# The first norm's weights as one row, spread over the partitions by TensorE

## The chip, the cores and the metric

The kernel runs on one core of one Trainium2 chip. The metric is the device time of one execution in microseconds (us), the median of several runs. The program is a whole two-layer encoder in float32; the change concerns its first 25 us.

## The reference

A trunk of two layers over 256 tokens of width 1,024. Ahead of the layers stands a layer norm with a weight and a bias per feature; each layer is a token mixer (one input projection, four groups of heads, one output projection) and a channel mixer (dense, then eight experts), each followed by a norm.

```python
def layer_norm(x, w, b):
    xf = x.astype(jnp.float32)
    mu = jnp.mean(xf, -1, keepdims=True)
    var = jnp.mean(jnp.square(xf - mu), -1, keepdims=True)
    y = (xf - mu) * lax.rsqrt(var + EPS) * w.astype(jnp.float32) + b.astype(jnp.float32)
    return y.astype(x.dtype)
...
    h = layer_norm(x, ln_in_w, ln_in_b)
    for l in range(DEPTH):
        mix = token_mixer(h, w_in[l], w_out[l], ...)
        h = layer_norm(DN_ALPHA * h + mix, ln1_w[l], ln1_b[l])
...
        h = layer_norm(DN_ALPHA * h + f, ln2_w[l], ln2_b[l])
    return h
```

## The kernel before

Each engine has its own program, written out by hand in one order; semaphores join them. `x` is two tiles of 128 tokens by 1,024 features, `h[:, t, :]`.

**The queue.** All loads of the start are issued by SP, one behind the other, with no wait between them: the two tiles of `x`, the first norm's weights (`load_ln(0)`: `lnb`, 128 partitions by 2,048 columns, 1,024 KB; the host has repeated the row of 1,024 weights and 1,024 biases for all 128 partitions), the identity (`cst[:, first]`, 64 KB), the first block of input weights (`load_win(0, 0)`, 2,048 KB), the parameters (`pr`), a part of the constants, the second block of input weights (`load_win(0, 1)`), the rest of the constants, and the third block.

**The first norm** (`layer_norm(0, ...)` on VectorE). Statistics of both tiles (`stats`, L1581 to L1584); GpSimd turns each variance into 1/deviation (L516). Then, for tile 0 and then tile 1: the centre, two instructions of 512 columns, h = (h - mean) * weight (L1595), and the scale, one of 1,024 columns, h = h * (1/deviation) + bias (L1599), which signals `h_ready`. Every later norm (n = 1 to 4) goes through the same code.

**TensorE** waits for the identity and then runs `keep_busy(10, 7)`, ten products of the identity with itself into a corner of bank 7, whose results nobody reads (the fillers, L527). Then `transposes_of_h(0)` (L551): for each tile, as soon as its `h_ready` is there, eight 128x128 transposes into two PSUM banks, `HT_BANK[0] + 2 * t` and the next; with `HT_BANK[0] = 0` these are banks 0 to 3. ScalarE copies each bank to `hT` (L1224, four copies). Then `mix_0()`: it waits for all four copies and runs `unit(0, 0)` (L619, 16 products of 256 columns with the first block of input weights, into bank 5), `unit(0, 8)` (L631 and L632: for each of eight slices a product with the 16 gate columns and one of 512 columns with the second block, into banks 4 and 6), and so on. A product in float32 has two records in the trace, one for each pass of its weights.

**ScalarE**, after its four copies, waits for the parameters and starts the chain of small instructions of the S5 group (L1230).

Of the kernel before, what the change touches and what calls it, by code (L numbers as in the profile page):

```python
# [15 lines left out]
ALU = mybir.AluOpType  # L16
# [4 lines left out]
D = 1024  # L21
# [35 lines left out]
WOUT_LOADS = ((1, 2), (2, 7))  # L57
OUT_ORDER = (3, 2, 0, 1)
TILES = ((0, 1), (1, 0), (0, 1), (1, 0), (0, 1))
HT_BANK = (0, 4, 0, 0)  # L60
LINE = 64
MAGIC = 12582912.0
TURN = 6.2831850
# [4 lines left out]
def columns(sizes):  # L68

    at, out = 0, {}  # L70
    for name, n in sizes:
        out[name] = (at, at + n)
        at += n
    return out, -(-at // LINE) * LINE


CONST, CONST_W = columns([
    ("decay", H * 3 * P), ("dft_c", 512), ("dft_s", 512), ("idft_c", 512), ("idft_s", 512),
    ("window", 512), ("rot_c", 128), ("rot_s", 128), ("mask_fw", P), ("mask_bw", P), ("before", P),
    ("iota", P), ("ident", P), ("ones", P), ("pos", 2 * L), ("pick", H * P),  # L80
    ("m0", 2), ("nm0", 2), ("halfpi", 1), ("lower", NE * NE)])
# [7 lines left out]
def trunk(nc, x, ln, const, par, w_in, w_out, ffn, moe, tab, out):  # L89
    ctx = ExitStack()  # L90
    with ctx:
        place_of = {}

        def sb(name, shape, dt=F32):
            tensor = ctx.enter_context(nc.sbuf_tensor(name, shape, dt))
            place_of[name] = nc.sbuf_base - 4 * math.prod(shape[1:])
            assert name in ("lead", "over") or place_of[name] % (4 * LINE) == 128
            return tensor

        def sem(name):  # L100
            return ctx.enter_context(nc.semaphore(name))
# [8 lines left out]
        h = sb("h", [P, TT, D])  # L110
        lnb = sb("lnb", [P, 2 * D])
# [43 lines left out]
        bank = [ctx.enter_context(nc.psum_tensor(f"bank{i}", [P, 512], F32)) for i in range(8)]  # L155

        def K(name, rows=P):
            a, b = CONST[name]
            return cst[0:rows, a:b]
# [5 lines left out]
        ident = K("ident")  # L165
# [63 lines left out]
        def sm(a, n):  # L229
            return small[:, a:a + n]  # L230

        mv = sm(0, 4).rearrange("p (t s) -> p t s", t=2)
        bst = sm(4, 24).rearrange("p (t c s) -> p t c s", t=2, c=2)
        var, rstd = sm(28, 2), sm(30, 2)
# [23 lines left out]
        s_id, s_cst, s_par, s_ln = sem("identity_in"), sem("const_in"), sem("params_in"), sem("ln_in")  # L258
# [7 lines left out]
        dch, ach, pch = sem("dve_chain"), sem("act_chain"), sem("pool_chain")  # L266
        ln_var, ln_rstd, h_ready, ht_ps, ht_ready = (
            sem("ln_var"), sem("ln_rstd"), sem("h_ready"), sem("ht_transposed"), sem("ht_ready"))
        mix_ready = sem("residual_psum")
        init = sem("init_done")  # L270

# [55 lines left out]
        def ln_home(n):  # L327

            return ret[:, :] if n == 2 else lnb[:, :]
# [34 lines left out]
        def _(sp):  # L364
# [26 lines left out]
            def load_ln(n):  # L391
                if n == 2:
                    sp.wait_ge(f_pm, 2)
                    sp.wait_ge(f_sq, 4)
                elif n == 4:
                    sp.wait_ge(e_uu, 2 * NC_E * 6)
                elif n:
                    sp.wait_ge(h_ready, 2 * n)
                sp.dma_start(ln_home(n), ln[n]).then_inc(s_ln, 16)

            for t in range(TT):
                sp.dma_start(h[:, t, :], x[t * P:(t + 1) * P, :]).then_inc(s_x[t], 16)
            load_ln(0)
            first = slice(*CONST["ident"])
            sp.dma_start(cst[:, first], const[:, first]).then_inc(s_id, 16)
            load_win(0, 0)
            sp.dma_start(pr[:, :], par[0]).then_inc(s_par, 16)
# [78 lines left out]
            for c in range(2):  # L486
                sp.wait_ge(o_ready, 2 + c)
                part = slice(c * 512, (c + 1) * 512)
# [32 lines left out]
        def _(pe):  # L521
            mm, tr = nc.tensor.matmul, nc.tensor.transpose

            def keep_busy(count, b):

                for _ in range(count):
                    mm(bank[b][:, 384:512], ident, ident, start=True, stop=True)  # L527
# [11 lines left out]
            def transposes_of_h(n):  # L539
                for i, t in enumerate(TILES[n]):  # L540
                    if n == 1 and i:
                        keep_busy(6, 4)
                    elif n == 3 and i:
                        keep_busy(5, 7)
                        logits(0)
                        keep_busy(7, 7)
                    pe.wait_ge(h_ready, 2 * n + i + 1)
                    for j in range(2):
                        for q in range(4):
                            k = 4 * j + q  # L550
                            ins = tr(bank[HT_BANK[n] + 2 * t + j][:, q * P:(q + 1) * P], h[:, t, k * P:(k + 1) * P],  # L551
                                     ident)
                        ins.then_inc(ht_ps, 1)
                    if n == 1:
                        pe.wait_ge(d_id, 1)
                        for hf in range(2):
                            mm(bank[2 * t + hf][:, :], alpha_id, h[:, t, hf * 512:(hf + 1) * 512],
                               start=True, stop=False)
# [487 lines left out]
                    pre(1, k)  # L1046

            pe.wait_ge(s_id, 16)
            keep_busy(10, 7)
            transposes_of_h(0)  # L1050
            mix_0()
            transposes_of_h(1)
# [154 lines left out]
        def _(ac):  # L1207
# [7 lines left out]
            def evacuate_h(n):  # L1215
                dst = ff_x[0] if n == 1 else hT
                for i, t in enumerate(TILES[n]):
# [4 lines left out]
                    for j in range(2):  # L1222
                        ac.wait_ge(ht_ps, 4 * n + 2 * i + j + 1)
                        act(dst[:, 4 * j:4 * j + 4, t * P:(t + 1) * P],  # L1224
                            bank[HT_BANK[n] + 2 * t + j][:, :].rearrange("p (q n) -> p q n", q=4), ACT.Copy
                            ).then_inc(ht_ready, 1)
# [339 lines left out]
        def _(ve):  # L1566
            tt, ts, stt = nc.vector.tensor_tensor, nc.vector.tensor_scalar, nc.vector.scalar_tensor_tensor
            count = [0]

            def link(ins):  # L1570

                count[0] += 1
                ins.then_inc(dch, 1)
                ve.wait_ge(dch, count[0])

            def layer_norm(n, src, ready):

                def stats(i, t):
                    for c in (OUT_ORDER[2 * i] % 2, OUT_ORDER[2 * i + 1] % 2) if n % 2 else range(2):
                        ready(i, t, c)  # L1580
                        ins = nc.vector.bn_stats(bst[:, t, c, :], src(t, c))  # L1581
                    link(ins)
                    link(nc.vector.bn_aggr(mv[:, t, :], bst[:, t].rearrange("p c s -> p (c s)")))
                    ts(var[:, t:t + 1], mv[:, t, 1:2], EPS, None, ALU.add).then_inc(ln_var, 1)  # L1584

                for i, t in enumerate(TILES[n]):
                    if n or i == 0:
                        stats(i, t)
                    if n == 0 and i == 0:
                        stats(1, TILES[0][1])  # L1590
                    if i == 0:
                        ve.wait_ge(s_ln, 16 * (n + 1))
                    for c in range(2):
                        part = slice(c * 512, (c + 1) * 512)
                        ins = stt(out=h[:, t, part], in0=src(t, c), scalar=mv[:, t, 0:1], in1=ln_home(n)[:, part],  # L1595
                                  op0=ALU.subtract, op1=ALU.mult)
                    link(ins)
                    ve.wait_ge(ln_rstd, 2 * n + i + 1)
                    stt(out=h[:, t, :], in0=h[:, t, :], scalar=rstd[:, t:t + 1], in1=ln_home(n)[:, D:2 * D],  # L1599
                        op0=ALU.mult, op1=ALU.add).then_inc(h_ready, 1)  # L1600

            def of(tensor):
                return lambda t, c: tensor[:, t, c * 512:(c + 1) * 512]
# [30 lines left out]
            def pre(l, k):  # L1634
# [27 lines left out]
                elif k < 11:  # L1662
                    j = k - 7
                    ve.wait_ge(f_spm, 4 * l + j + 1)
                    tt(spec[:, j // 2, j % 2, :], (bank[SPEC_BANK[j]] if l else pb[(j + 1) % 2])[:, :], rnorm, ALU.mult).then_inc(f_spec, 1)
                elif k == 11:
                    dt_, x1, th, tf, rr, _, sn, cs, n1, n2, n3 = s5v
                    ve.wait_ge(c_exp, 3 * l + 3)
                    tt(n1, rr, cs, ALU.mult)
# [401 lines left out]
            def ff_w2_lo(u, dst):  # L2071
# [3 lines left out]
                tt(dst[1][:, :], w2, dst[0][:, :].bitcast(F32), ALU.subtract).then_inc(d_mid, 1)  # L2075

            layer_norm(0, of(h), lambda i, t, c: ve.wait_ge(s_x[t], 16))
            for l in range(DEPTH):
                ve.wait_ge(ht_ready, 8 * l + 4)
                if l == 0:  # L2080
                    mix_0()
                else:
                    mix_1()
                layer_norm(2 * l + 1, of(h), mixed(l))
                if l == 0:
                    ff_up_lo(0, 0)
                    for j in range(2):
                        for i, t in enumerate(TILES[1]):
                            ve.wait_ge(ht_ready, 4 + 2 * i + j + 1)
                            k, c = 4 * j, t * P  # L2090
                            tt(ff_x[1][:, k:k + 4, c:c + P],
                               bank[HT_BANK[1] + 2 * t + j][:, :].rearrange("p (q n) -> p q n", q=4),
                               ff_x[0][:, k:k + 4, c:c + P].bitcast(F32), ALU.subtract).then_inc(d_x, 1)
                    ff_up_lo(0, 1)
                    for u in range(2 * NC_FF):
# [20 lines left out]
                        elif u == max(PRE1) + 2:  # L2116
                            pre_norm(1)
                    layer_norm(2, lambda t, c: bank[2 * t + c][:, :], dense_done)
                    for k in range(7, 11):
                        pre(1, k)  # L2120
# [329 lines left out]
```

## Time and profile before

| | us |
|---|---|
| median of 3 runs | 1655.72 |
| lowest, highest | 1655.27, 1655.87 |
| the profiled execution, its own time | 1655.2 |
| its span, first to last instruction | 1653.3 |
| TensorE matmul busy in it | 1608.9 |
| VectorE busy in it | 1356.2 |

The span is some 1.9 us shorter than the execution's time, so a time is compared with a time and a span with a span. PE is TensorE's matmul, PEld its weight load, which runs beside it; DVE is VectorE, ACT ScalarE, POOL GpSimd, SP the engine that issues the loads. L with a number is a line of the kernel.

### The profile page before, as it was taken

Reading aid. Unit: us, or ns where it says so; the run is one execution under the profiler, and the core shown is the slowest. Engines: PE = TensorE matmul, PEld = TensorE weight load, DVE = VectorE, ACT = ScalarE, POOL = GpSimd, SP = SyncE. Lnnn points to the kernel's source line nnn. Section 1 sums busy time; section 2 is a strip of 40 time slices with the busy share of each in tenths; the row PEclk is TensorE's granted clock in tenths of the full one; section 3 lists DMA queues with packets and bytes.
Section 4 is the critical chain, followed back from the end, with each engine's and each line's share of the span. In section 5 each row is a group of like instructions: output and inputs, shape, how many; then the busy total and the mean of one; then the engine's idle time right before and its main releaser. Section 6 shows DMA issues by size and latency. Waiting matters only on the chain.

```text
span 1653.3 us, 18582 instructions
## 1 busy us (share of the span) xinstructions
PE 1608.9 (97%) x7608; PEld 1261.2 (76%) x7608; DVE 1356.2 (82%) x1447; ACT 945.5 (57%) x961; POOL 52.5 (3%) x39
## 2 busy tenths in 40 slices
PE   7997999999999999999999999999999999999996
PEld 5645759988856766788888888888888888888885
DVE  6899467775667947888988998989989889998898
ACT  4321326654312133877777777767777777777773
POOL 0111000000011100000000000000000000000000
PEclk9999999999999999999999999999999999999998
DMA  7230153663523134899989999989999989999981
GB/s 324 102 144 9 77 221 154 238 246 128 219 76 139 52 146 185 311 373 371 368 339 354 363 362 372 357 346 352 363 364 373 360 344 352 384 364 375 361 333 46
DMA packets 40604, 444.24 MB, mean 269 GB/s; under 512 B 4416, under 2 KB 4544, under 8 KB 7360
## 3 DMA queue, kind: packets, MB, share of 16 engines
q1 hardware_dynamic: 39360, 438.78, 68.0%
q10 hardware_dynamic: 1152, 4.19, 0.6%
q8 instruction: 62, 1.02, 0.2%
q14 instruction: 30, 0.25, 0.0%
HBM read 437.71 MB, written 5.24 MB: 268 GB/s over the span
## 4 chain that ended last, share of the span: by engine, by line
PE 86%; DVE 9%; ACT 3%; DMA 1%; issue 1%; SPq 0%; DVEq 0%; ACTq 0%
PE bank L1132 34%; PE bank L1159 16%; PE bank L1021 8%; PE bank L619 5%; PE bank L632 4%; PE bank L1031 4%; PE bank L828 3%; DVE ring_lo L2062 1%; PE bank L1140 1%; DVE ring_lo L2201 1%; PE bank L790 1%; DMA win<-w_in 1%; ACT ex_up_hi L1431 1%; PE bank L527 1%; PE bank L1080 1%
## 5 line engine op out<-in xcount | busy, mean ns | idle before, releaser
L2062 DVE TENSOR_TENSOR ring_lo<-ring,ex_up_hi 128x2048 fp32r<-128x2048 f32 x224 | 512.9, 2290 | 51.4 <-ACT ex_up_hi L1431 49.9
L1431 ACT ACTIVATE ex_up_hi<-ring 128x2048 fp32r<-128x2048 f32 x224 | 429.2, 1916 | 106.1 <-PE bank L1132 106.1
L1132 PE MATMUL bank<-ex_up_hi,ex_x_hi 128*128 128x512 f32 x896 | 362.4, 404 | 5.5 <-DVE ring_lo L2062 4.7
L1132 PE MATMUL bank<-ring_lo,ex_x_hi 128*128 128x512 f32 x896 | 350.7, 391 | 0.0
L1132 PE MATMUL bank<-ex_up_hi,ex_x_lo 128*128 128x512 f32 x896 | 349.9, 391 | 0.0
L2201 DVE TENSOR_TENSOR ring_lo<-ring,ex_w_hi 128x2048 fp32r<-128x2048 f32 x111 | 253.1, 2281 | 0.0
L1550 ACT ACTIVATE ex_w_hi<-ring 128x2048 fp32r<-128x2048 f32 x111 | 211.4, 1905 | 0.0
L1132 PEld LDWEIGHTS bank<-ex_up_hi,ex_x_hi 128*128 128x128 f32 x896 | 168.3, 188 | 43.7 <-DVE ring_lo L2062 12.1
L1132 PEld LDWEIGHTS bank<-ring_lo,ex_x_hi 128*128 128x128 f32 x896 | 168.2, 188 | 36.6
L1132 PEld LDWEIGHTS bank<-ex_up_hi,ex_x_lo 128*128 128x128 f32 x896 | 168.8, 188 | 30.6
L1159 PE MATMUL bank<-ex_w_hi,ex_mid_hi 128*128 128x512 f32 x448 | 174.5, 389 | 0.0
L1159 PE MATMUL bank<-ring_lo,ex_mid_hi 128*128 128x512 f32 x448 | 174.3, 389 | 0.0
L1159 PE MATMUL bank<-ex_w_hi,ex_mid_lo 128*128 128x512 f32 x448 | 174.3, 389 | 0.0
L1021 PE MATMUL bank<-ff_x_hi,ff_up_hi 128*128 128x256 f32 x352 | 100.8, 286 | 0.0
L1021 PE MATMUL bank<-ff_x_hi,ff_up_lo 128*128 128x256 f32 x352 | 99.6, 283 | 0.0
L1021 PE MATMUL bank<-ff_x_lo,ff_up_hi 128*128 128x256 f32 x352 | 99.6, 283 | 0.0
L1159 PEld LDWEIGHTS bank<-ex_w_hi,ex_mid_hi 128*128 128x128 f32 x448 | 84.1, 188 | 17.7 <-DVE ring_lo L2201 0.2
L1159 PEld LDWEIGHTS bank<-ring_lo,ex_mid_hi 128*128 128x128 f32 x448 | 84.1, 188 | 17.5
L1159 PEld LDWEIGHTS bank<-ex_w_hi,ex_mid_lo 128*128 128x128 f32 x448 | 84.1, 188 | 17.4
L632 PE MATMUL bank<-win,hT 128*128 128x512 f32 x192 | 91.4, 608 | 0.0
L1544 ACT ACTIVATE sc<-bank 128x256 f32<-128x256 f32 x112 | 43.0, 384 | 84.2 <-PE bank L1132 84.2
L619 PE MATMUL bank<-hT,win 128*128 128x256 f32 x384 | 86.0, 382 | 1.6 <-ACT hT L1224 1.6
(339 smaller groups left out, 2094.5 us busy)
## 6 DMA issues: line engine op xcount, KB each, us to landing
ring<-moe SPq DMA_DIRECT2D x112, 2048.0 KB, 7.6
ring<-moe SPq DMA_DIRECT2D x112, 1024.0 KB, 7.4
ring<-ffn SPq DMA_DIRECT2D x11, 3072.0 KB, 10.2
win<-w_in SPq DMA_DIRECT2D x12, 2048.0 KB, 8.3
win<-w_out SPq DMA_DIRECT2D x4, 2048.0 KB, 10.4
lnb<-ln SPq DMA_DIRECT2D x4, 1024.0 KB, 5.8
tab<-yT ACTq DMA_DIRECT2D x8, 512.0 KB, 5.8
pr<-par SPq DMA_DIRECT2D x2, 1728.0 KB, 11.8
```

The costliest lines, as they stand in the source:

```text
L619: ins = mm(b[:, q * L:(q + 1) * L], w[:, k, c:c + P], hT[:, k, :], start=(k == 0), stop=(k == KT - 1))
L632: ins = mm(b[:, :], x, w[:, k, :], start=(k == 0), stop=(k == KT - 1))
L828: ins = mm(bank[b][:, :], yT[:, k, t * P:(t + 1) * P], w[:, k, :], start=(n == 0 and i == 0), stop=(n == 3 and i == 1))
L1021: ins = mm(bank[4 + u % 2][:, w * L:(w + 1) * L], ff_up[j][:, w, k, :], ff_x[i][:, k, :], start=(k == 0 and n == 0), stop=(k == KT - 1 and ...
L1031: ins = mm(bank[2 * t + hf][:, :], ff_mid[i][:, u % 2, t * P:(t + 1) * P], w2[j][:, hf * 512:(hf + 1) * 512], start=False, stop=(u == NU - ...
L1132: ins = mm(b[:, :], ex_x[x % 3][x_][:, k, :], (ex_up_hi, lo)[w_][:, k, :], start=(k == 0 and m == 0), stop=(k == KT - 1 and m == 2))
L1159: ins = mm(bank[2 * (x % 2) + hf][:, :], ex_mid[a][:, g % 2, f * P:(f + 1) * P], w2[b], start=(c == 0 and f == 0 and m == 0), stop=(c == N ...
L1431: act(ex_up_hi[:, HS * q:HS * (q + 1), :], wt[:, HS * q:HS * (q + 1), :], ACT.Copy).then_inc(e_uh, 1)
L1544: act(sil[g % 2], bank[4 + g % 2][:, 0:L], ACT.Silu).then_inc(e_sil, 1)
L1550: act(ex_w2_hi[g % 2][:, :], ring[here][:, UPW:SLOT], ACT.Copy).then_inc(e_wh, 1)
L2062: tt(ring_lo[s][:, half], ring[s][:, half], hi.bitcast(F32), ALU.subtract).then_inc(e_ul, 1)
L2201: tt(ring_lo[s][:, UPW:SLOT], ring[s][:, UPW:SLOT], ex_w2_hi[g % 2][:, :].bitcast(F32), ALU.subtract).then_inc(e_wl, 1)
```

## The change

The host's array of norm weights stays as it is, but for the first norm only its first row is loaded, 8 KB onto partition 0 of `lnb`. The load of the identity is widened to the identity and the ones (the constant `ones` lies next to it), 128 KB in place of 64. TensorE waits for both and multiplies a row of 128 ones with each 512 columns of the row, four products with a contraction over one row; so banks 0 and 1 hold the weights on all partitions, banks 2 and 3 the biases. A new semaphore, `ln_rows`, counts them. Eight fillers follow in place of ten. The first norm's transposes move to banks 4 to 7. On VectorE both tiles' centres come first, with the third operand from banks 0 and 1, and then both scales, each cut into two instructions of 512 columns, with the biases from banks 2 and 3. The later norms are as before.

```diff
-HT_BANK = (0, 4, 0, 0)
+HT_BANK = (4, 4, 0, 0)
...
-            load_ln(0)
-            first = slice(*CONST["ident"])
+            first = slice(CONST["ident"][0], CONST["ones"][1])
+            sp.dma_start(lnb[0:1, :], ln[0][0:1, :]).then_inc(s_ln, 16)
             sp.dma_start(cst[:, first], const[:, first]).then_inc(s_id, 16)
             load_win(0, 0)
...
             pe.wait_ge(s_id, 16)
-            keep_busy(10, 7)
+            pe.wait_ge(s_ln, 16)
+            for q in range(4):
+                mm(bank[q][:, :], K("ones", 1), lnb[0:1, q * 512:(q + 1) * 512], start=True, stop=True).then_inc(ln_rows, 1)
+            keep_busy(8, 7)
             transposes_of_h(0)
...
-                for i, t in enumerate(TILES[n]):
-                    if n or i == 0:
-                        stats(i, t)
-                    if n == 0 and i == 0:
-                        stats(1, TILES[0][1])
-                    if i == 0:
-                        ve.wait_ge(s_ln, 16 * (n + 1))
+                def centre(t):
                     for c in range(2):
                         part = slice(c * 512, (c + 1) * 512)
-                        ins = stt(out=h[:, t, part], in0=src(t, c), scalar=mv[:, t, 0:1], in1=ln_home(n)[:, part],
-                                  op0=ALU.subtract, op1=ALU.mult)
+                        ins = stt(out=h[:, t, part], in0=src(t, c), scalar=mv[:, t, 0:1],
+                                  in1=ln_home(n)[:, part] if n else bank[c][:, :], op0=ALU.subtract, op1=ALU.mult)
                     link(ins)
...
+                if n == 0:
+                    a, b = TILES[0]
+                    stats(0, a)
+                    stats(1, b)
+                    ve.wait_ge(ln_rows, 2)
+                    centre(a)
+                    centre(b)
+                    ve.wait_ge(ln_rows, 4)
+                    for i, t in enumerate((a, b)):
+                        ve.wait_ge(ln_rstd, i + 1)
+                        for c in range(2):
+                            part = h[:, t, c * 512:(c + 1) * 512]
+                            ins = stt(out=part, in0=part, scalar=rstd[:, t:t + 1], in1=bank[2 + c][:, :],
+                                      op0=ALU.mult, op1=ALU.add)
+                        ins.then_inc(h_ready, 1)
```

## Rows read from the trace of the kernel before

**Rows 1.** The page, busy time of each engine and its share.

```profile
PE 1608.9 (97%) x7608; PEld 1261.2 (76%) x7608; DVE 1356.2 (82%) x1447; ACT 945.5 (57%) x961; POOL 52.5 (3%) x39
```

**Rows 2.** The chain that ended last, first 27 us: start, us, what.

```profile
4.45 19.63 DMA win<-w_in
24.12 0.40 PE bank L631 x2
24.51 0.95 PE bank L632 x2
```

**Rows 3.** Timeline of TensorE, in several windows: start, us, operation, idle time before.

```profile
8.62 4.48 PE L527 MATMUL bank<-cst 128*128 128x128 f32 x20 [8.62 <-DMA cst<-const]
...
11.12 1.97 PE L527 MATMUL bank<-cst 128*128 128x128 f32 x9
...
12.19 0.91 PE L527 MATMUL bank<-cst 128*128 128x128 f32 x4
12.94 0.71 PE L551 MATMUL bank<-cst,h 128*128 128x128 f32 x5
...
15.69 7.17 PE L619 MATMUL bank<-hT,win 128*128 128x256 f32 x32 [0.74 <-ACT hT L1224]
24.12 0.40 PE L631 MATMUL bank<-pr,hT 128*128 128x16 f32 x2 [1.25 <-DMA win<-w_in]
```

**Rows 4.** The chain that ended last, further on.

```profile
44.00 7.06 PE bank L632 x16
...
60.55 7.10 PE bank L619 x32
...
86.69 0.69 DVE yT L1653
...
147.25 1.11 PE bank L644 x4
```

**Rows 5.** Timeline of VectorE.

```profile
4.64 1.29 DVE L1581 BATCH_NORM_STATS2 small<-h 128x6 f32<-128x512 f32 x2 [4.64 <-DMA h<-x]
...
6.28 1.28 DVE L1581 BATCH_NORM_STATS2 small<-h 128x6 f32<-128x512 f32 x2
...
7.83 0.15 DVE L1584 TENSOR_SCALAR small<-small 128x1 f32<-128x1 f32 x1
8.42 1.42 DVE L1595 SCALAR_TENSOR_TENSOR h<-h,small,lnb 128x512 f32<-128x512 f32 x2 [0.43 <-DMA lnb<-ln]
9.87 1.28 DVE L1599 SCALAR_TENSOR_TENSOR h<-h,small,lnb 128x1024 f32<-128x1024 f32 x1
11.07 1.41 DVE L1595 SCALAR_TENSOR_TENSOR h<-h,small,lnb 128x512 f32<-128x512 f32 x2
12.51 1.28 DVE L1599 SCALAR_TENSOR_TENSOR h<-h,small,lnb 128x1024 f32<-128x1024 f32 x1
```

**Rows 6.** Timeline of ScalarE.

```profile
13.57 2.06 ACT L1224 ACTIVATE hT<-bank 128x512 f32<-128x512 f32 x4 [11.55 <-PE bank L551]
17.63 0.22 ACT L1230 ACTIVATE small<-pr 128x16 f32<-128x16 f32 x1 [1.99 <-DMA pr<-par]
```

**Rows 7.** Windows: length, busy of PE, PEld, DVE, ACT, POOL, then granted clock, DMA share, GB/s.

```profile
6.00:8.00 2.00, 0.00 (x0) 0.00 (x0) 1.88 (x6) 0.00 (x0) 0.54 (x1) 1.00 1.08 437
...
10.00:11.00 1.00, 1.00 (x7) 1.00 (x6) 1.00 (x1) 0.00 (x0) 0.00 (x0) 1.00 1.03 442
...
13.00:14.00 1.00, 1.00 (x10) 0.88 (x9) 0.80 (x1) 0.43 (x1) 0.00 (x0) 1.00 1.00 429
```

**Rows 8.** Timeline of the queue that issues the loads.

```profile
0.74 0.87 SPq L402 DMA_DIRECT2D h<-x  x2
1.66 0.42 SPq L399 DMA_DIRECT2D lnb<-ln  x1
2.12 0.43 SPq L405 DMA_DIRECT2D cst<-const  x1
```

**Rows 9.** Instructions that read the constants before 20 us: ns, least/median/most.

```profile
L527 PE MATMUL bank<-cst x20: 274/421/580, 8.6 to 12.8; 128*128 128x128 f32 x20
```

**Rows 10.** Lines L1610 and L1595 over the whole span: ns, least/median/most.

```profile
L1610 DVE SCALAR_TENSOR_TENSOR h<-h,bank x8: 670/684/689, 227.7 to 640.7; 128x512 f32<-128x512 f32 x8
...
L1595 DVE SCALAR_TENSOR_TENSOR h<-h,small,lnb x12: 740/746/752, 8.4 to 643.1; 128x512 f32<-128x512 f32 x12
L1595 DVE SCALAR_TENSOR_TENSOR h<-bank,small,ret x4: 741/741/742, 439.9 to 444.8; 128x512 f32<-128x512 f32 x4
```

**Rows 11.** Windows around 150 us, columns as in rows 7.

```profile
142.00:146.00 4.00, 0.00 (x0) 0.00 (x0) 3.90 (x6) 0.00 (x0) 1.70 (x1) 0.99 0.00 0
146.00:150.00 4.00, 2.75 (x13) 2.75 (x14) 4.00 (x5) 1.58 (x2) 0.65 (x1) 0.50 0.00 0
150.00:153.00 3.00, 3.00 (x8) 2.42 (x8) 2.97 (x7) 0.30 (x1) 0.00 (x0) 0.54 0.00 0
```

**Rows 12.** Timeline of TensorE there.

```profile
147.25 1.11 PE L644 MATMUL bank<-cst,cv 128*128 128x128 f32 x4 [5.31 <-DVE cv L1776]
```

More of the change, by code:

```diff
@@ L268, in trunk @@
             sem("ln_var"), sem("ln_rstd"), sem("h_ready"), sem("ht_transposed"), sem("ht_ready"))
+        ln_rows = sem("ln_in_row_on_all_partitions")
         mix_ready = sem("residual_psum")
@@ L1597, in layer_norm @@
                     link(ins)
-                    ve.wait_ge(ln_rstd, 2 * n + i + 1)
-                    stt(out=h[:, t, :], in0=h[:, t, :], scalar=rstd[:, t:t + 1], in1=ln_home(n)[:, D:2 * D],
-                        op0=ALU.mult, op1=ALU.add).then_inc(h_ready, 1)
+                for i, t in enumerate(TILES[n]):
+                    if n:
+                        stats(i, t)
+                        if i == 0:
+                            ve.wait_ge(s_ln, 16 * (n + 1))
+                        centre(t)
+                        ve.wait_ge(ln_rstd, 2 * n + i + 1)
+                        stt(out=h[:, t, :], in0=h[:, t, :], scalar=rstd[:, t:t + 1], in1=ln_home(n)[:, D:2 * D],
+                            op0=ALU.mult, op1=ALU.add).then_inc(h_ready, 1)
```

## Prediction

> **What bounds the kernel now.** The page comes first: TensorE is busy nearly all of the span [rows 1], so a microsecond taken off the front of TensorE's work should come off the end, and nothing else in the start counts. So I read the chain of work that ended last in its first 27 us. It doesn't pass through the norm at all: up to 24.12 it is the DMA of the second block of input weights, and from there TensorE [rows 2]. The first block's product (unit 0, L619) began at 15.69 and was over at 22.86; then TensorE stood 1.25 us until that block landed [rows 3]. So two things race for 24.12: the DMA queue and the norm with unit 0 behind it; the norm loses by some 1.3 us. The chain after that is TensorE without a gap up to 86.69 and VectorE from there to 147.25 [rows 4], so what happens to the start at 24.12 happens to the end.
>
> Next the norm itself, on VectorE's timeline: the statistics end at 7.98, the first centre starts at 8.42 when the norm's weights land (0.43 us idle), and each tile takes 1.45 us for its centre (8.42 to 9.87) and 1.20 to 1.28 for its scale. The last scale ends at 13.79 [rows 5]. From there to unit 0 it is 15.69 - 13.79 = 1.90 us: the second tile's transposes and two evacuations [rows 3, 6].
>
> **What is removed from the queue.** 1,024 KB of norm weights go and 8 KB come; the load of the identity grows from 64 to 128 KB. That is 952 KB less. The DMA engines are full at 437 GB/s between 6 and 8 us [rows 7], so what stands behind is 0.975 MB / 437 GB/s = 2.23 us earlier: the identity at 8.62 - 2.23 = 6.39 instead of 8.62 [rows 3], the second weight block at 24.12 - 2.23 = 21.89, the parameters at 17.63 - 2.23 = 15.40 [rows 6]. The one-row load is ahead of the identity in the same queue; it is issued at the time of the old one, 1.66 [rows 8]. Its own price isn't in the trace; its bounds are nothing and 0.3 us. A first load needs 4.64 - 0.74 = 3.9 us from issue to first use [rows 5, 8], and issued at 1.66 that would be 5.56, before 6.39; but if one of the 16 engines carried the whole row, it would be busy 8.2 KB / (437/16 GB/s) = 0.3 us with it, and its share of the identity later by as much. I take nothing, the nearer one, since the row could be spread. Lower end for TensorE's start: 6.0, since the second x load must be through (its statistics start at 6.28 without waiting [rows 5]). So the start is 6.39, with 6.0 to 6.7 as its range. The queue's gain is no gain for the end by itself: the best that it can give is 24.12 - 21.89 = 2.23 us, if unit 0 were over by then, and unit 0 ends at 22.86 even now.
>
> **What is added on TensorE.** Four products of 512 columns with one row of weights. Before them TensorE has done nothing. The nearest rows are the first fillers, 128 columns each and two records to one: records start 0.214 us apart ((12.19 - 11.12)/5), and from 12.94 transposes of the same size start 0.109 us apart ((0.71 - 0.27)/4 [rows 3]): that is 1.2 GHz for some 3.9 us after the first instruction, 2.4 GHz after. The granted clock reads 1.00 over both [rows 7]; here the durations decide. A cold product of 512 columns is then 4 x 2 x 0.214 = 1.71 us; a warm one is 7.06/8 = 0.88 (16 records of L632 [rows 4]). The first two are cold: 6.39 + 0.15 for the slow first record (its 580 ns against 421 of the others [rows 9]) + 2 x 1.71 + 0.21 until the last record is through (421 - 214 ns) = 10.17. If the clock rises 3.9 us after the start again, at 10.3, the third costs 0.34 + 0.80 x 0.88 = 1.04 and the fourth 0.88, so TensorE is done issuing at 11.9 and the result is there at 12.1. The eight fillers run at 2.4 GHz then, 16 x 0.109 = 1.7 us, over by 13.6. They are not on the path: the transposes wait for VectorE later than that.
>
> The page of the Trainium skill "TensorE: Matmul & The Clock Gate", section "What's actually happening", says that 1.2 GHz is the resting clock and that activity releases it. The trace agrees in this one start: records 0.214 us apart from 8.62 on, 0.109 from 12.94. By that rule the products would do the fillers' service and the sum stays. The same page, section "Part 4: PE-mode transpose", says that transposes don't count as busy in the way that other products do; of products with one row it says nothing. That rule would leave the sum as it is too, and is a part of the third rival.
>
> **What moves on VectorE.** The centres no longer wait for a transfer at 8.42 but for two products at 10.17: 1.75 us later. Both centres first: 2 x 1.45 = 2.90, to 13.07. The scales wait for products three and four, at 12.1: hidden by the centres, with 1 us to spare. The scales are cut into two halves each: two of 512 columns cost 0.67 + 0.75 = 1.42 in place of 1.28 (the centre's pair [rows 5]), so the first is ready at 14.49, and the second, started 0.08 before the first's end, at 15.83. That the third operand comes from a PSUM bank I cost at nothing: this instruction with a bank as operand has taken 741 ns (L1595) and 684 (L1610) against 746 from SBUF [rows 10]. The last scale is 15.83 - 13.79 = 2.04 us later than now. With the same 1.90 us behind it unit 0 starts at 17.73, and 7.10 of issue later [rows 4] TensorE is free at 24.83. The weights have been there since 21.89. So the second unit starts at 24.83 and not at 24.12: **0.7 us later**.
>
> **What is hidden.** ScalarE's parameter work (L1230) waits for its load until 17.63 now [rows 6]; after, it waits for its own evacuations, over at about 17.7: no change. The reordered order of centre and scale delays the first tile's transposes (from 12.8 to 14.5), but the second tile's decide. SP issues the same number of loads. The other banks for the transposes (4 to 7) cost nothing: the filler's writes into bank 7 are ahead of them on the same engine, and the first unit waits for all four evacuations as now.
>
> **Sum against the profile.** The profiled execution took 1655.2 us with a span of 1653.3; +0.7 gives 1655.9 and 1654.0. The median of the runs is 1655.72, 0.5 above the profiled one, so the prediction is 1655.72 + 0.7 = 1656.4. About 0.2%, 3.3 us, is what a measurement of this kernel can tell from no change.
>
> **Rivals.** (1) *The queue wins.* If the rows were on all partitions by 9.4 (a start at 6.0 and the first two products partly at the higher clock), the last scale would be at most 1.25 us later and the weights' wait of now would swallow it: 0, and 22.86 - 24.12 = -1.3 if it weren't later at all. For it: the wait of 1.25 us is real. Against: no row shows anything at the higher clock within 3.9 us of the first instruction. Time 1654.4 to 1655.9. A gain over 2.2 us can't come from this place.
>
> (2) *The clock rises late.* If it rises at 12.9 as in the trace of now, and not 3.9 us after the start, the fourth product ends at 13.3 and the scales start 0.2 later: +0.9. If one-row products do not raise it at all, the four end at 6.54 + 6.85 + 0.21 = 13.6, the eight fillers run from 13.4 to 16.8 at 0.214 a record, the transposes come after them and not after VectorE, and TensorE warms at 17.3. Sixteen transpose records, some of them cold, to 18.8, 0.9 more for the last evacuation, unit 0 from 19.7: +2.7 us, 1658.4.
>
> (3) *Slower by more than can be missed: the same, and the transposes don't raise it either.* Then neither the products nor the eight fillers bring the rise before the transposes, as in the trace ten did, and unit 0 starts at about 21.1 (16 records at 0.214, then 0.9) and runs its first 4 us at half speed: free at 30.2, +6 us, 1661.8. It decides, past +3.3, as soon as a good part of unit 0 itself runs cold. (The Trainium skill's page on TensorE speaks for its second half, as quoted; the trace can't tell, since the transposes of now came after the rise.) For it: ten fillers had run when the clock rose, now there are eight, behind work of which no row shows whether it raises the clock. Against: TensorE is busy from 6.4 without a break, as before from 8.6.
>
> (4) *Something further on.* TensorE's granted clock falls to half between 146 and 153 us, after 5.3 us without work, and about 5.5 us of work lie in it [rows 11, 12]. If everything comes 0.7 us later, that stretch may cost up to half of 5.5 less or more: +0.7 - 2.7 = -2.0 or +3.4, 1653.7 or 1659.1. Against: three runs within 0.6 us say that it falls alike each time.
>
> **How the numbers follow.** Chances: forecast (+0.2 to +1.2) 0.58; the queue wins 0.13; late clock (+1.2 to +3.3) 0.15; cold unit 0 (over +3.3) 0.06; something further on 0.08, of which 0.03 past +3.3 and 0.02, for what I don't see, past -3.3. So faster by over 0.2% has 0.02, slower 0.06 + 0.03 = 0.09, within it 0.89. The range leaves out some 1 in 10 at either side: it goes down to 1654.8, into the first rival, and up to 1658.6, which takes in the second one's 1658.4 and what a median may be off.
>
> **What would show it.** In the profile after: four products (eight records) of 512 columns at 6.4, the first pairs 1.71 us each; a wait of VectorE before the first centre until 10.2, ended by TensorE and not by a DMA, and none before the first scale; the last scale's end at 15.8; unit 0 at 17.7; and no idle time before the first product with the gates (L631), at 24.8. I am wrong on the sign if that product starts before 24.1. I am wrong on the mechanism if the fillers' records are 0.214 apart, or if VectorE waits before its scales.

## Result and profile after

| | us |
|---|---|
| before, median of 21 runs | 1655.72 (1654.29 to 1657.41) |
| changed, median of 21 runs | 1658.59 (1656.59 to 1659.20) |
| ratio | 1.0016, 95% interval 1.0011 to 1.0022 |
| changed, profiled execution and its span | 1658.54 and 1656.6 |

The change costs 2.9 us, 0.16 to 0.17%. That is inside the range that was forecast (1654.8 to 1658.6, 0.01 below its upper end) and within 0.2%, but it isn't the likeliest case of 1656.4: it is the second half of the second rival, which had 1658.4.

The first rows to read are TensorE's timeline of the changed kernel, the counterpart of [rows 3]:

```profile
6.24 7.19 PE L1052 MATMUL bank<-lnb,cst 1*128 1x512 f32 x8 [6.24 <-DMA cst<-const]
13.36 3.78 PE L528 MATMUL bank<-cst 128*128 128x128 f32 x16
16.94 2.12 PE L552 MATMUL bank<-cst,h 128*128 128x128 f32 x16
19.90 7.17 PE L620 MATMUL bank<-hT,win 128*128 128x256 f32 x32 [0.84 <-ACT hT L1228]
26.91 0.29 PE L632 MATMUL bank<-pr,hT 128*128 128x16 f32 x2
```

The products start at 6.24 (forecast 6.39): the shorter queue has done its part. But their eight records take 7.19 us, some 1.7 a product to the last one. Behind them the sixteen records of the eight fillers take 3.78 us, 0.224 apart ((3.78 - 0.42)/15): still 1.2 GHz. So the transposes start at 16.94 and not when VectorE has the first tile. The gates' first product (L632) starts at 26.91 in place of 24.12, with no wait for its weights.

The source view of the products' line says the same for each record (least, median, most in ns):

```profile
L1052 PE MATMUL bank<-lnb,cst x8: 1056/1056/1217, 6.2 to 12.4; 1*128 1x512 f32 x8
```

All are alike, so the clock did not rise between 6.2 and 13.4, and the first four records are no dearer than the last four. VectorE's timeline, the counterpart of [rows 5]:

```profile
10.06 2.85 DVE L1593 SCALAR_TENSOR_TENSOR h<-h,small,bank 128x512 f32<-128x512 f32 x4 [2.17 <-PE bank L1052]
13.53 2.72 DVE L1618 SCALAR_TENSOR_TENSOR h<-h,small,bank 128x512 f32<-128x512 f32 x4 [0.63 <-DVE h L1593]
```

The centres wait 2.17 us for two products and start at 10.06 (forecast 10.17); the scales, which should not have waited at all, wait 0.63. The row puts that down to VectorE's own last centre. That had long been done: it is the wait for the fourth product, whose last record ended at 12.4 + 1.06 = 13.4. The last scale ends at 13.53 + 2.72 = 16.25 (before: 13.79), the first tile was ready at about 14.9; TensorE came to it 2 us later.

The chain that ended last ran through the DMA queue before [rows 2]. Now it runs from the load of the identity and the ones through TensorE's products, fillers and transposes and ScalarE's copies; VectorE's norm isn't in it:

```profile
2.02 4.17 DMA cst<-const
6.24 7.19 PE bank L1052 x8
13.43 3.71 PE bank L528 x16
17.15 0.61 PE bank L552 x4
17.78 2.07 ACT hT L1228 x4
19.90 7.17 PE bank L620 x32
```

Products and fillers together are 10.9 us of it. The fillers, work whose result nobody reads, are on the path for 3.7 of them.

Three more lines of the profile after bear on the rest of the 3.3 us between the two spans. The windows around 150 us, the counterpart of [rows 11], with the granted clock as the third number from the end:

```profile
137.00:140.00 3.00, 3.00 (x8) 1.19 (x8) 2.97 (x6) 0.00 (x0) 0.00 (x0) 0.50 0.03 5
...
150.00:153.00 3.00, 2.99 (x14) 2.66 (x15) 3.00 (x5) 1.88 (x2) 0.00 (x0) 0.58 0.00 0
153.00:157.00 4.00, 4.00 (x11) 3.19 (x10) 3.96 (x8) 0.00 (x0) 0.00 (x0) 0.50 0.00 0
```

The stretch at half the clock behind the gap is there as before, a little later against the work in it, and a second one lies at 137. The second costs nothing here: TensorE waits for VectorE behind it, and the product after that wait starts at 149.94 (before: 147.25 [rows 12]), 2.69 later, which is what the first 27 us give. The other 0.6 of the 3.3 arises after it. Experiments 7 and 8 size the stretch behind the gap.

### The profile page after: what moved, and what is told of

It is laid out like the page before. It is cut to its first block, busy times and chain, and to the rows that moved or that the text cites. A ratio compares the mean times of both kernels' runs of the same rounds, so it can differ in the third digit from the quotient of the medians.

```text
span 1656.6 us, 18592 instructions
## 1 busy us (share of the span) xinstructions
PE 1617.2 (98%) x7612; PEld 1264.3 (76%) x7612; DVE 1355.6 (82%) x1449; ACT 945.1 (57%) x961; POOL 52.4 (3%) x39
## 4 chain that ended last, share of the span: by engine, by line
PE 87%; DVE 9%; ACT 3%; issue 1%; DMA 0%; SPq 0%; DVEq 0%; ACTq 0%
PE bank L1136 34%; PE bank L1163 16%; PE bank L1022 8%; PE bank L620 5%; PE bank L633 4%; PE bank L1032 4%; PE bank L829 3%; DVE ring_lo L2082 1%; PE bank L1144 1%; DVE ring_lo L2221 1%; PE bank L791 1%; PE bank L528 1%; ACT ex_up_hi L1435 1%; PE bank L1084 1%; PE bank L653 1%
## 5 line engine op out<-in xcount | busy, mean ns | idle before, releaser
L1163 PEld LDWEIGHTS bank<-ex_w_hi,ex_mid_lo 128*128 128x128 f32 x448 | 84.1, 188 | 17.4
```

Of the source, the lines that this page charges most:

```text
L1163: ins = mm(bank[2 * (x % 2) + hf][:, :], ex_mid[a][:, g % 2, f * P:(f + 1) * P], w2[b], start=(c == 0 and f == 0 and m == 0), stop=(c == N ...
```

## Experiments

The theory from the profile: **a product with a contraction over one row does not raise TensorE's clock**, and so the four products are at 1.2 GHz to the last, and so are the fillers behind them. Rivals: the long products with few weight loads don't raise it; or it was the moment of the start. For each run the time is told as a median against that of the kernel before on the same chip, with the ratio and its 95% interval; an interval that takes in 1 doesn't tell the two apart. "Gates" is the start of the gates' first product in the run's profile: 24.12 before, 26.91 in the change. That start is read from one execution and the loads vary: in kernels with the old queue the second block landed at 24.0 to 25.0.

### 1. The products over 128 rows

```diff
+            nc.vector.memset(lnb[:, :], 0.0).then_inc(pre_set, 1)
...
+            sp.wait_ge(pre_set, 1)
             sp.dma_start(lnb[0:1, :], ln[0][0:1, :]).then_inc(s_ln, 16)
...
-                mm(bank[q][:, :], K("ones", 1), lnb[0:1, q * 512:(q + 1) * 512], ...)
+                mm(bank[q][:, :], K("ones"), lnb[:, q * 512:(q + 1) * 512], ...)
```

> The changed kernel with its four products contracted over 128 rows instead of one: VectorE zeroes the norm's row tile at the start, the row lands on partition 0 of it after that, and the weights are ones on all 128 partitions; everything else is as in the changed kernel. In the profile of the change the records of the four products stay 0.85 us apart for 7.1 us and the fillers behind them 0.214 us. Theory (products with one row don't raise TensorE's clock): here it rises some 4 us after the first product, so that from the third or fourth on the records are 0.44 us apart, the fillers 0.109, and the first product with the gates (L632) starts at about 24.8 instead of 26.91: +0.7 us against the kernel before. Rival (it is the long products with few weight loads, or the moment at which the start falls, and rows don't matter): the same as the change, 26.9 and +2.8 us.

Measured: 1655.13 against 1655.60, ratio 1.0000 (0.9991 to 1.0009). Gates at 24.30. TensorE's timeline, and the source view of the products:

```profile
5.97 6.14 PE L1054 MATMUL bank<-lnb,cst 128*128 128x512 f32 x8 [5.97 <-DMA cst<-const]
11.96 1.95 PE L530 MATMUL bank<-cst 128*128 128x128 f32 x16
14.14 0.55 PE L554 MATMUL bank<-cst,h 128*128 128x128 f32 x3 [0.24 <-DVE h L1622]
```

```profile
L1054 PE MATMUL bank<-lnb,cst x8: 592/1061/1222, 6.0 to 11.5; 128*128 128x512 f32 x8
```

The last records take 592 ns and not 1,056, the fillers 1.95 us and not 3.78, and the transposes wait for VectorE (0.24 us) and not for the fillers. Nothing but the number of rows has changed on TensorE (the added rows hold zeros), and 2.6 us of the 2.8 are gone. The theory holds, and long products don't hinder the rise. The rise came later than forecast, though: the products take 5.99 us from their start to the first filler, where 5.5 were reckoned; with 0.854 us for a cold record and 0.44 for a warm one that puts it at some 4.9 us after the start and not 3.9. VectorE's centres hid the difference.

### 2. The fillers of the kernel before over one row

```diff
-            keep_busy(10, 7)
+            for _ in range(10):
+                mm(bank[7][:, 384:512], cst[0:1, a:b], cst[0:1, a:b], start=True, stop=True)
```

with a:b the identity's columns.

> The kernel before with its ten fillers contracted over one row instead of 128, same columns and same number; nothing of the change is in it. Theory (one row doesn't raise the clock): the fillers are 0.214 us apart to the end, the transposes too (3.4 us for 16 in place of 1.9), unit 0 starts at about 17.2 and runs its first 2 to 4 us at 0.43 us a record; the gates' first product comes at 26 to 28 instead of 24.12, +2 to +4 us. Rival (rows don't matter): the transposes 0.109 us apart, unit 0 at 15.7, no change.

Measured: 1657.03 against 1655.60, ratio 1.0009 (1.0000 to 1.0018). Gates at 27.09.

```profile
9.22 4.63 PE L1050 MATMUL bank<-cst 1*128 1x128 f32 x20 [9.22 <-DMA cst<-const]
13.78 3.67 PE L551 MATMUL bank<-cst,h 128*128 128x128 f32 x16
18.14 9.11 PE L619 MATMUL bank<-hT,win 128*128 128x256 f32 x32 [0.69 <-ACT hT L1225]
27.09 0.29 PE L631 MATMUL bank<-pr,hT 128*128 128x16 f32 x2
```

The transposes take 3.67 us; at the 0.109 a record of the kernel before sixteen take 2.0. Unit 0 takes 9.11 for 7.17 [rows 3]. So one-row products are no use as fillers in a kernel that has nothing of the change in it. The price by the medians is +1.4, at the edge of what the interval tells from nothing, and the gates' start is 3.0 later, of which 0.6 is a later identity (9.22 for 8.62). The two belong to different executions: the profiled one took 1657.84 us, 2.6 more than the profiled one of the kernel before (1655.2) and 0.8 more than its own median. So the rows, more than the median, carry this experiment.

### 3. Early fillers over a tile that needs no load

```diff
+            nc.vector.memset(sc[:, 0:128], 1.0).then_inc(pre_set, 1)
...
+            pe.wait_ge(pre_set, 1)
+            for _ in range(12):
+                mm(bank[7][:, 384:512], sc[:, 0:128], sc[:, 0:128], start=True, stop=True)
             pe.wait_ge(s_id, 16)
```

> The changed kernel with twelve fillers more, from about 1 us on, over a tile that VectorE sets at the start, so before any load is there; the products keep their one row. Theory (the extra time of the change is the clock's): the fillers end at about 6.1 with the clock up or nearly so, the four products are 0.88 us each instead of 1.71, VectorE starts its centres at 8.2 to 8.5, and the gates' first product starts at about 23.0: 1.1 us less than the kernel before, 3.9 less than the change. Rival (the rise needs something else, or the products let it fall again): products at 1.71 us and +0.7 to +2.8 us.

Measured: 1656.33 against 1655.60, ratio 1.0003 (0.9994 to 1.0012). Gates at 24.68: neither the gain that I expected nor the price of the change. The timeline, the source view of the products and the windows (granted clock third from the end) tell why:

```profile
1.05 4.85 PE L1052 MATMUL bank<-sc 128*128 128x128 f32 x24 [1.05 <-DVE sc L1578]
6.13 4.89 PE L1056 MATMUL bank<-lnb,cst 1*128 1x512 f32 x8 [0.22 <-DMA cst<-const]
10.95 3.78 PE L529 MATMUL bank<-cst 128*128 128x128 f32 x16
```

```profile
L1056 PE MATMUL bank<-lnb,cst x8: 587/640/1052, 6.1 to 10.0; 1*128 1x512 f32 x8
```

```profile
5.00:8.00 3.00, 2.78 (x13) 1.61 (x12) 2.76 (x8) 0.00 (x0) 0.56 (x2) 1.00 1.00 389
8.00:11.00 3.00, 3.00 (x6) 0.73 (x4) 2.81 (x4) 0.00 (x0) 0.62 (x3) 0.58 0.99 423
11.00:15.00 4.00, 4.00 (x20) 4.00 (x20) 2.72 (x4) 0.00 (x0) 0.00 (x0) 0.50 0.98 419
15.40:18.00 2.60, 1.75 (x15) 1.49 (x14) 0.16 (x2) 2.16 (x5) 0.00 (x0) 1.00 1.13 479
```

The early fillers do bring the clock up, and the first two products run at 2.4 GHz (records from 587 ns on), the last at 1.2 (up to 1,052). Then, while TensorE is busy 3.00 of 3.00 us with one-row products, the granted clock falls from 1.00 to 0.58 and stays at 0.50 until past 15 us, 4 us after the fillers behind began. This is the sharpest of the readings: here the profile itself names the clock, and it falls in the middle of uninterrupted work, at about 8.5 (0.58 is the mean of 8 to 11), 2.4 us after the first one-row product. Whether the 0.22 us without work ahead of the products had a part in it is what the fifth experiment tests. (In the other starts the column reads 1.00 where the durations say 1.2 GHz, as in [rows 7]; the first change of the clock that the profiler notes seems to be what it knows.)

### 4. The queue alone

```diff
+            nc.vector.memset(lnb[:, 0:D], 1.0).then_inc(s_ln, 8)
+            nc.vector.memset(lnb[:, D:2 * D], 0.0).then_inc(s_ln, 8)
...
-            load_ln(0)
```

> The kernel before without the load of the first norm's weights: VectorE sets them to 1 and 0 on all partitions before the first load lands, so the first norm is one without weight and bias. No products, nothing moved. It gives what the shorter queue is worth by itself. Expected: all that stood behind the load lands 1.05 MB / 437 GB/s = 2.4 us earlier; the norm starts 0.43 us earlier, at 7.98; unit 0 is over at about 22.4 and the second block of weights lands at 21.7, so the gates' first product starts at 22.4: -1.7 us. If the second block were still late the rival is -1.7 as well at most; if nothing changes, the queue was not what held that product.

The first norm of this kernel leaves out the weight and the bias. Measured: 1654.62 against 1655.60, ratio 0.9992 (0.9983 to 1.0001). The gates' product, and what TensorE did first:

```profile
6.02 4.63 PE L526 MATMUL bank<-cst 128*128 128x128 f32 x20 [6.02 <-DMA cst<-const]
10.44 1.79 PE L550 MATMUL bank<-cst,h 128*128 128x128 f32 x8
...
22.51 0.40 PE L630 MATMUL bank<-pr,hT 128*128 128x16 f32 x2 [0.45 <-DMA win<-w_in]
```

The gates are 1.6 us earlier than before, and the load is still the last to arrive. So 1.6 us is what the shorter queue bought at the gates with nothing to spread. In the medians it is 1.0, which the interval doesn't tell from nothing, and the profiled execution took 1655.33, no less than the profiled one of before. The 1.6 us were still there at 145.66, where the product behind the gap starts (before: 147.25). They went in a stretch at half the clock that before doesn't have at this place; the windows at 558 us, first of before, then of this run:

```profile
558.00:562.00 4.00, 4.00 (x18) 3.24 (x18) 3.93 (x8) 0.00 (x0) 0.00 (x0) 1.00 0.00 0
558.00:562.00 4.00, 4.00 (x11) 3.23 (x12) 3.92 (x7) 0.00 (x0) 0.00 (x0) 0.57 0.00 0
```

Of this run 558 to 562 reads 0.57 with TensorE busy throughout: that is 3.4 us at half speed, by which I estimate 1.7 us lost. A single execution can lose by that as much as the change is about.

The first two rows show something else. The fillers here have 128 rows, and yet TensorE ran at 1.2 GHz from 6.02 until about 12.0: the eight transposes from 10.44 on are still 0.213 apart ((1.79 - 0.30)/7). The time from the first product to the rise isn't fixed.

### 5. Both cures

The edits of 1 and 3 together; VectorE sets the fillers' tile first, then zeroes the row's, and the row's load waits for both.

> Both cures together: the changed kernel with products over 128 rows (the first experiment) and with twelve fillers from about 1 us on (the third). Theory (one-row products count for TensorE's clock as if it stood still): the fillers bring the clock up at 5 to 6 us as they did in the third experiment, and now it stays up: the four products are 1.76 us a pair, over by 9.8; the centres start at 8.1, the last scale ends at 13.7, unit 0 starts at 15.6, the gates' first product at 22.7 instead of 24.12: -1.4 us against the kernel before, -4.2 against the change. Rival (the fall of the clock at 8.4 in the third experiment came from the load's wait or from something else than the rows): products 3 and 4 at 1.71 us again and 24.5 or later.

Measured: 1654.85 against 1655.68, ratio 0.9997 (0.9988 to 1.0007). Gates at 23.55.

```profile
5.93 3.70 PE L1057 MATMUL bank<-lnb,cst 128*128 128x512 f32 x8 [0.46 <-DMA cst<-const]
9.47 1.95 PE L530 MATMUL bank<-cst 128*128 128x128 f32 x16
...
15.45 7.17 PE L622 MATMUL bank<-hT,win 128*128 128x256 f32 x32 [0.74 <-ACT hT L1233]
23.55 0.39 PE L634 MATMUL bank<-pr,hT 128*128 128x16 f32 x2 [0.92 <-DMA win<-w_in]
```

All four products at 2.4 GHz (3.70 us for eight records), unit 0 at 15.45. With the third experiment's fillers and a gap of 0.46 us for 0.22, and the rows changed, the clock doesn't fall: the rival of that run is out too. Now the load is the later one again: the zeroing holds the row's load back until 3.17, and what stands behind it. By the medians the gain is 0.8 us, which the interval doesn't tell from nothing.

### 6. The change without its fillers

```diff
-            keep_busy(8, 7)
             transposes_of_h(0)
```

> The changed kernel without the eight fillers behind the products. In the change they stand on the path: they run from 13.36 to 16.7, and VectorE had the first tile ready at 14.9. Theory (neither one-row products nor transposes raise the clock): the transposes run from 14.9 at 0.214 us a record, to 18.4, unit 0 starts at 19.3 and its first 3 to 4 us or more run at 0.43 a record, so the gates' first product comes at 28.3 or later: +1.4 us or more against the change, +4.2 against the kernel before. Rival (transposes raise it): the clock is up at 18.9, unit 0 runs at 0.216 a record throughout and the gates' product comes at 26.3, 0.6 us less than the change.

Measured: 1659.12 against 1655.68, ratio 1.0019 (1.0010 to 1.0028). Gates at 29.04.

```profile
15.42 3.68 PE L552 MATMUL bank<-cst,h 128*128 128x128 f32 x16 [1.56 <-DVE h L1617]
19.78 9.42 PE L620 MATMUL bank<-hT,win 128*128 128x256 f32 x32 [0.69 <-ACT hT L1227]
```

The transposes now wait for VectorE, but they and the first ten records of unit 0 run at 1.2 GHz. So the fillers on the path gave back at least their 3.7 us: without them the gates come 2.1 us later than in the change, 0.4 of it from a later start of the products (6.66 for 6.24). By the medians it is +3.4 against the kernel before where the change has +2.9; those intervals overlap.

### 7 and 8. The clock behind 142 us taken out of both kernels

```diff
+                keep_busy(20, 1)
                 hyena_transposes(0, 1)
```

in the kernel before (7) and in the changed one (8).

> The kernel before with 20 fillers at 142 us, where TensorE stands 5.3 us waiting for VectorE ahead of the second transposes of the Hyena group; 4.4 us of them fit in. With e8 it takes away what the clock does after that gap, so that the difference of the two is that of the first 25 us alone. Expected: no stretch at half the granted clock behind 147, -1 to -2.7 us; if the clock was already down when they start they take up to 8.7 us and it is +1 to +2.

> The changed kernel with the same 20 fillers. If the change costs what its first 25 us say, this is 2.8 us above e7 (the gates' first product at 26.91 instead of 24.12); if a part of the 2.9 us of the medians came from the clock at 147 us, less or more.

Measured: (7) 1655.15, ratio 1.0000 (0.9991 to 1.0009); (8) 1657.95, ratio 1.0015 (1.0006 to 1.0024), both beside 1655.68. In the windows of (8) the clock is up again where it was at 0.50 and 0.58:

```profile
146.00:151.00 5.00, 5.00 (x46) 4.95 (x45) 4.90 (x8) 0.00 (x0) 2.36 (x1) 1.00 0.00 0
151.00:157.00 6.00, 6.00 (x34) 4.92 (x33) 5.96 (x10) 1.88 (x2) 0.00 (x0) 1.00 0.00 0
```

The difference of the two medians is 2.80 us, that of the two kernels as they are 2.87; each is uncertain by some 1 us or more. The profiles are closer: the gates start at 24.01 and 27.28, 3.3 apart, since the identity of (8) came at 6.90, and the two executions took 1653.77 and 1657.09, again 3.3 apart. So the price of the change is made in the first 27 us, and no part of the clock at 147 is seen in it. Taking that stretch away is worth 0.5 us by the medians where I expected 1 to 2.7, and the interval of (7) doesn't tell that from nothing.

### 9 and 10. The version that should beat both

As 5, with the zeroing shared: GpSimd zeroes one half of the tile (`nc.gpsimd.memset(lnb[:, D:2 * D], 0.0)` ahead of its first instruction) and VectorE the other. Run 10 has the 20 fillers of 7 besides.

> The fifth experiment (128 rows, early fillers) with the zeroing of the row's tile shared: VectorE zeroes the half for the weights (it took 1.76 us for all of it), GpSimd the half for the biases. In the fifth the queue stood until 3.17 for it, and the second weight block landed at 23.55, 0.9 us after unit 0 was over, against 22.51 in the fourth, whose queue never waited. Expected: the row's load is issued at about 2.3, the second block lands at about 22.7, and the gates' first product starts there: -1.4 us against the kernel before. If GpSimd is slow at it (no row shows this size on GpSimd) the queue waits longer and it is the fifth again or worse.

> The same with the 20 fillers at 142 us of the seventh experiment. If the two gains add, -1.4 and -0.5 to -1: 1653.5 or so, clear of the kernel before; the clock's stretch at half speed behind 147 us is gone in the rows.

Measured: (9) 1653.90 against 1655.50, ratio 0.9988 (0.9979 to 0.9997); (10) 1653.62, ratio 0.9989 (0.9979 to 0.9998). Both are below the kernel before, by 1.6 and 1.9 us, with intervals that end just short of 1, and 4.5 to 4.8 below the change, each by way of the kernel before. The row's load is issued at 2.10. The products and the gates of (9), then the gates of (10):

```profile
6.94 3.70 PE L1059 MATMUL bank<-lnb,cst 128*128 128x512 f32 x8 [1.36 <-DMA cst<-const]
...
23.46 0.31 PE L636 MATMUL bank<-pr,hT 128*128 128x16 f32 x2
```

```profile
23.32 0.40 PE L636 MATMUL bank<-pr,hT 128*128 128x16 f32 x2 [0.45 <-DMA win<-w_in]
```

The gates' starts, 23.46 and 23.32, are not the 22.7 that I expected, nor better than the 23.55 of the fifth: in (9) the identity came at 6.94, a microsecond after the fifth's, and in (10) the second block at 23.3. Whether sharing the zeroing bought anything isn't shown; the medians of 5 and 9 lie 1 us apart with runs that spread over 2. Nor is it shown that the fillers of 7 add anything in (10).

### 11. Transposes as fillers

```diff
-            keep_busy(10, 7)
+            for _ in range(10):
+                tr(bank[7][:, 384:512], ident, ident)
```

> The kernel before with its ten fillers made transposes of the identity: same columns, same records, 128 rows. The second and sixth experiments had the clock still down after 3.7 us of transposes, but with a gap of 0.7 to 1.1 us behind them. Theory (transposes don't raise the clock either): fillers and transposes all at 0.214 us a record, unit 0 starts at about 17.2 and runs its first 3.5 us or more at 0.43 a record; the gates' product at 26 to 28, +1.4 to +3 us as in the second. Rival (they do, and the gap decided there): the rise some 4 us after the first filler, as before, and no change.

Measured: 1656.40 against 1655.50, ratio 1.0006 (0.9996 to 1.0015).

```profile
9.53 2.40 PE L1050 MATMUL bank<-cst 128*128 128x128 f32 x10 [9.53 <-DMA cst<-const]
...
12.12 1.82 PE L551 MATMUL bank<-cst,h 128*128 128x128 f32 x8 [0.19 <-DVE h L1600]
...
14.76 1.10 PE L551 MATMUL bank<-cst,h 128*128 128x128 f32 x8 [0.82 <-DVE h L1600]
16.60 7.17 PE L619 MATMUL bank<-hT,win 128*128 128x256 f32 x32 [0.74 <-ACT hT L1225]
```

The expectation has the same number of records; but a transpose has one and not two, so these fillers last half as long. Eight transposes of the first tile take 1.82 us, those of the second 1.10, and unit 0 runs at full speed from its start: the clock rose at 13.7, 4 us after the first filler, when TensorE had done nothing but transposes (the first tile's are 0.22 apart, (1.82 - 0.27)/7, the second's 0.12). So my theory on transposes is wrong. What held the clock down in runs 2 and 6 was not shown. Both had 3.7 us of transposes and then a gap of 0.69, where this one had two lots of them with 0.19 between. But nothing special need have held it: the fourth experiment took some 6 us from its first filler to the rise, with 4.4 of them products over 128 rows, so 3.7 us without a rise say nothing against transposes.

## Why the likeliest case was wrong

**Right.** That the chain of before passed through the queue and not through the norm, with 1.3 us between; what the shorter queue gives (the products at 6.24 for a forecast 6.39; with nothing to spread 1.6 us at the gates, where 2.2 was the most); a cold product's 1.71 us; the two-product wait (10.06 for 10.17); banks as operands at no price (2.85 us for four, as from SBUF); the sign, and that it is less than 0.2%.

**The step that failed** is in "What is added on TensorE": "If the clock rises 3.9 us after the start again, at 10.3". It didn't rise, since the products have one row. Everything after hangs on it. The third and fourth product cost some 1.7 each in place of 1.04 and 0.88, so the scales started at 13.53 and not at 13.07; that alone is 0.5 us. And the fillers cost 3.7 in place of 1.7 and began at 13.4 in place of 11.9, so the transposes waited for them and not for VectorE: unit 0 at 19.90 for 17.73, and the gates at 26.91 for 24.83. Where the rows are 128, as in the first experiment, the forecast's world is there: scales at 12.7, unit 0 at 17.29, gates at 24.30, 0.5 better than forecast since its start was 0.4 earlier.

**The 3.9 us in that step.** They were read a little short: from 12.19 to 12.94 four records start in 0.75 us [rows 3], which is three at 0.214 and one at 0.109, so the clock of before rose at some 12.8, 4.2 after the first filler. And one start is no measure of the others. By the same sum, for work over 128 rows, it is some 3.2 us in the fifth experiment (24 records of fillers in 4.42 us), 4.9 in the first and 6 in the fourth. In the change the clock rose at some 17.4, 11 us after the first product but 4.0 after the first filler: that is outside this scatter if the one-row products count, and inside it if they don't.

**The rival that came true** is the second half of (2), "if one-row products do not raise it at all": transposes after the fillers at 16.8 (16.94), unit 0 from 19.7 (19.90), +2.7 (+2.87). It had 0.15 together with a milder case, against 0.58 for the likeliest. That the measured time lies in the range is due to the range having been drawn up to 1658.6 so as to take this rival in; with 1658.59 it is also luck. The trace of before had no one-row product ahead of which the clock was down, so it couldn't decide; my "against", that TensorE would be busy without a break, took busy time for what raises the clock. The third rival is out: the clock was up when unit 0 began. The fourth has no part that experiments 7 and 8 can see, though in the profiled execution of the change 0.6 us of the 3.3 arose behind the gap. The rule that I weighed from the Trainium skill ("TensorE: Matmul & The Clock Gate", "What's actually happening"), that activity releases the throttle, doesn't say which activity; experiments 1 to 3 and 5 bound it. The eleventh, with the clock up at 13.7 after nothing but transposes, speaks against what the same page of the Trainium skill says in "Part 4: PE-mode transpose", that transposes don't count as busy in the same way; the page's times there are for bf16, here it was float32.

## What to carry to other kernels

In these runs a product over one row filled TensorE's time and was idleness to its clock: spreading a row over the partitions in this way, at a start, ran at half speed and left the work behind it at 1.2 GHz. Zero the other partitions and contract over all of them: that costs TensorE no more, but the zeroing has its own price, 1.76 us of VectorE ahead of the row's load, which held it back by 1.4 to 1.5 us in the first and fifth experiment (issued at 3.03 and 3.17 for 1.66). How many rows are enough was not measured. Fillers that need a loaded operand start when the load is there; over a tile that an engine sets itself they had the clock up before the products began in experiments 3, 5, 9 and 10. When a load is taken off a queue, look at what it was racing: here there were 1.3 us to win, and the work put in its place was on the other side of the race.

## What the runs showed of the hardware

- Four products of 512 columns over one row, 7.1 us without a break, left the clock at 1.2 GHz (the change); the same over 128 rows saw it rise within 5 us of the first (first experiment, records from 1,061 ns down to 592). With the clock up, one-row products let the granted clock fall from 1.00 to 0.58 and 0.50 while TensorE was busy all the time (third); the same over 128 rows didn't (fifth, eight records in 3.70 us).
- From the first product over 128 rows to the rise it took from some 3.2 us (fifth) to some 6 us (fourth) of work at 1.2 GHz.
- Transposes alone raised the clock (eleventh: up at 13.7 after transposes from 9.53 on).
- The granted clock can read 1.00 at a start where the durations say 1.2 GHz: 1.00 between 10 and 11 us of before, with records 0.214 us apart [rows 3, 7]. Why isn't shown.
